# A hybrid trunk layer in two passes over its tokens: a mixer step's pieces over more slots, a transposition behind the product's other riders, and the first pass's blocks of h split by VectorE alone

## What is computed

```python
h = rmsnorm(x, g_pre) * (1.0 + scale) + shift      # scale, shift, gate from c @ w_ada
p = h @ w_in                                       # 8704 output columns
# columns of p feed four token mixers, their gate paths and the merge gates
y_pool, y_hgrn, y_conv, y_diff = ...               # pooling, HGRN2 recurrence, short conv, differential attention
merged = sum(gates[b] * (y[b] @ w_merge[b]) for b in range(4))
x + gate * rmsnorm(merged @ w_out, g_post)
```

## Time and profile before

| what | value |
|---|---|
| median of 3 runs (2573.1 to 2575.48) | 2574.45 us |
| the profiled execution | 2568.26 us |
| its span, first to last instruction | 2566.5 us |
| mean granted clock of TensorE | 0.962 |
| TensorE busy | 2284.2 us (89%) |
| VectorE busy | 1689.7 us (66%) |
| ScalarE busy | 1259.9 us (49%) |
| GpSimd busy | 1093.9 us (43%) |

### The profile page before, as it was taken

One profiled execution on the slowest core, in us unless ns is written; L12 is line 12 of the kernel. 1 busy time (PEld: TensorE's weight loads), 2 busy tenths in 40 slices (PEclk: granted clock), 3 DMA queues, 4 the chain that ended last, 5 costly groups with the idle time before them and its releaser, 6 DMA issues. The chain is left out here.

```text
span 2566.5 us, 35701 instructions
## 1 busy us (share of the span) xinstructions
PE 2284.2 (89%) x11572; PEld 1859.2 (72%) x11572; DVE 1689.7 (66%) x2872; ACT 1259.9 (49%) x2634; POOL 1093.9 (43%) x883
## 2 busy tenths in 40 slices
PE   3599999999989999998999999999999965989898
PEld 2487777777767777776887888777777744767676
DVE  6776666658888785547777777588888735344442
ACT  3454555535554545445666666445555343434341
POOL 1513323225664654323334333366566425243343
PEclk6799999999999999999999999999999988999999
DMA  6467544334433436453424242343343266576582
GB/s 224 142 201 226 152 131 130 111 96 140 124 112 110 124 103 202 135 155 95 129 79 118 80 117 63 117 128 113 111 129 111 93 213 184 148 208 175 154 223 63
DMA packets 351328, 350.85 MB, mean 137 GB/s; under 512 B 25904, under 2 KB 277168, under 8 KB 350128
## 3 DMA queue, kind: packets, MB, share of 16 engines
q1 hardware_dynamic: 351152, 348.66, 46.0%
HBM read 242.15 MB, written 106.43 MB: 136 GB/s over the span
## 5 line engine op out<-in xcount | busy, mean ns | idle before, releaser
L1622 PE MATMUL gb<-h_hi,w_hi 128*128 128x512 f32 x1904 | 785.8, 413 | 89.1 <-DVE o L1207 53.5
L1624 PE MATMUL gb<-h_hi,w_lo 128*128 128x512 f32 x1904 | 756.3, 397 | 0.0
L1623 PE MATMUL gb<-h_lo,w_hi 128*128 128x512 f32 x1904 | 754.2, 396 | 0.0
L1197 DVE TENSOR_TENSOR w_lo<-w,w_hi 128x512 fp32r<-128x512 f32 x340 | 304.7, 898 | 298.9 <-ACT w_hi L902 298.0
L1622 PEld LDWEIGHTS gb<-h_hi,w_hi 128*128 128x128 f32 x1904 | 365.5, 192 | 175.6 <-issue 98.6
L1624 PEld LDWEIGHTS gb<-h_hi,w_lo 128*128 128x128 f32 x1904 | 364.1, 191 | 80.5
L1623 PEld LDWEIGHTS gb<-h_lo,w_hi 128*128 128x128 f32 x1904 | 366.0, 192 | 66.5
L988 ACT ACTIVATE C_prob<-C_sc,C_negm 128x512 f32<-128x512 f32 (+3 forms) x320 | 198.8, 623 | 270.4 <-DVE C_negm L1290 269.0
L781 POOL TENSOR_TENSOR C_prob<-C_prob,C_cf 128x512 f32<-128x512 f32 (+3 forms) x160 | 161.3, 1027 | 344.3 <-DVE C_cf L1312 330.0
L918 ACT ACTIVATE o<-gb 128x512 f32<-128x512 f32 x272 | 161.3, 593 | 268.5 <-PE gb L1624 255.5
L902 ACT ACTIVATE w_hi<-w 128x512 fp32r<-128x512 f32 x340 | 212.0, 625 | 100.1 <-PE gb L1624 98.9
(11 more groups left out here) (231 smaller groups left out, 4118.2 us busy)
## 6 DMA issues: line engine op xcount, KB each, us to landing
w<-in_w_in_dram SPq DMA_DIRECT2D x136, 512.0 KB, 4.1
gT_scratch<-o SPq DMA_DIRECT2D x128, 256.0 KB, 2.8
D_gate<-gT_scratch SPq DMA_DIRECT2D x32, 1024.0 KB, 9.8
pT_scratch<-o SPq DMA_DIRECT2D x80, 256.0 KB, 2.9
C_qt<-qB_scratch SPq DMA_DIRECT2D x128, 128.0 KB, 2.9
C_ks<-kT_scratch SPq DMA_DIRECT2D x48, 256.0 KB, 4.8
A_x_all<-in_x_dram SPq DMA_DIRECT2D x16, 512.0 KB, 6.9
A_ada<-in_w_ada_dram SPq DMA_DIRECT2D x8, 1024.0 KB, 12.1
```

The source lines that it names most:

```text
L1197: tt(w_lo[n % RING][:, :, :], source(n), w_hi[n % RING][:, :, :].bitcast(F32), ALU.subtract).then_inc(wlo, 1)
L1622: mm(to, hi[:, k, :], h_hi[j][:, k, :], start=(fresh and k == 0), stop=False, skip_group_check=True)
L1623: mm(to, hi[:, k, :], h_lo[j][:, k, :], start=False, stop=False, skip_group_check=True)
L1624: last = mm(to, lo[:, k, :], h_hi[j][:, k, :], start=False, stop=(k == KH - 1), skip_group_check=True)
```

## The change

Three places are edited.

1. Mixers. `distances_x` is cut in two pieces and each runs over two slots (-7 and -6; -3 and -2); `decays_first` becomes two pieces at -4 and -3; `sigmoids` loses its last four scalings, which become `affine` at -10; the pooling sigmoid moves ahead of it. `level_decays` of the second head pair goes from -2 to -1, `query_decays` and `decays_second` from -1 to 0, `decay_queries` from 0 to 1, `advance_state` from 10 to 11, `pool_out` from 10 to 12 and its store from 11 to 13.
2. `turn_back` of the first half stands behind `values` and `turn`.
3. In the first half ScalarE evicts h11, h12 and h22, VectorE h21; VectorE makes all of t1 to t4 and all seven low parts, in the order 0, 1, 2, 3, 5, 4, 6; GpSimd does nothing for h. The products' own order stays.

```diff
+FIRST_ORDER = (0, 1, 2, 3, 5, 4, 6)
+
+EVICT_V = ((4, 5, 6, 7), (0, 1, 2, 3, 8, 9, 10, 11))
+EVICT_A = ((0, 1, 2, 3, 8, 9, 10, 11, 12, 13, 14, 15), (4, 5, 6, 7, 12, 13, 14, 15))
...
+
+        def hi_count(half, j, kk):
+            return 2 * (PER * half + (j if half else FIRST_ORDER.index(j))) + kk + 1
+
+        def lo_count(half, j, kk):
+            if half == 0:
+                return h_lo_v, hi_count(0, j, kk)
+            if j in LOW_BY_VECTOR:
+                return h_lo_v, 2 * (PER + LOW_BY_VECTOR.index(j)) + kk + 1
+            return h_lo_p, 2 * LOW_BY_POOL.index(j) + kk + 1
...
                     store_y(i, 4, yc, yc_ready, yc_stored)
-                i = mix_step(n, 11)
+                i = mix_step(n, 13)
                 if i is not None:
...
@@ -837,15 +859,6 @@
             sum_s3_s1(0)
             sum_s2(0)
             sum_s4(0)
-            for kk in range(2):
-                low(1, kk, 0, operand_part(1, kk))
-            for kk in range(2):
-                t3(0, kk)
-            for j in LOW_BY_POOL[1:]:
-                for kk in range(2):
-                    if j == 4:
-                        pool.wait_ge(t3_made, kk + 1)
...
                     pool_part(i)
-                i = mix_step(n, -1)
+                i = mix_step(n, 0)
                 if i is not None:
...
-                link(a(k_s[i % 2][:, :, :], in3[i % 2][:, 2:4, :], ACT.Sigmoid, scale=-1.0))
+                a(k_s[i % 2][:, :, :], in3[i % 2][:, 2:4, :], ACT.Sigmoid, scale=-1.0)
+                link(a(q_s[i % 2][:, :, :], in3[i % 2][:, 0:2, :], ACT.Sigmoid))
+
+            def affine(i):
+
                 for t in range(2):
                     a(f_s[:, t, :], f_s[:, t, :], ACT.Identity, scale=omlb[:, t:t + 1], bias=lb[:, t:t + 1])
-                    a(k_s[i % 2][:, t, :], k_s[i % 2][:, t, :], ACT.Copy, scale=omlb[:, t:t + 1])
-                a(q_s[i % 2][:, :, :], in3[i % 2][:, 0:2, :], ACT.Sigmoid).then_inc(sig_ready, 1)
+                for t in range(2):
+                    ins = a(k_s[i % 2][:, t, :], k_s[i % 2][:, t, :], ACT.Copy, scale=omlb[:, t:t + 1])
+                ins.then_inc(sig_ready, 1)
+
+            def pool_sigmoid(i):
...
@@ -1087,13 +1102,13 @@
                 root_x(0, t)
             for n in range(LEAD):
                 high(n)
-            for kk in range(2):
-                high_h(0, kk)
-            for q in range(4, 8):
+            act.wait_ge(mod_ready, 1)
+            for q in range(4):
                 evict(0, q)
-            for kk in range(2):
-                high_h(1, kk)
-            for q in range(12, 16):
+            for j in range(2):
+                for kk in range(2):
+                    high_h(j, kk)
+            for q in range(8, 16):
                 evict(0, q)
             for kk in range(2):
...
                     for kk in range(2):
-                        high_h(3 + n, kk)
+                        high_h(FIRST_ORDER[3 + n], kk)
                 for b, off in OUT_SLOT.items():
...
                 if i is not None:
+                    pool_sigmoid(i)
                     sigmoids(i)
+                i = mix_step(n, -10)
+                if i is not None:
+                    affine(i)
                 i = mix_step(n, 5)
...
                     key_decays(i)
-                for t, off in enumerate((-5, -2)):
+                for t, off in enumerate((-5, -1)):
                     i = mix_step(n, off)
                     if i is not None:
                         level_decays(i, t)
-                i = mix_step(n, -1)
+                i = mix_step(n, 0)
                 if i is not None:
...
 
-            def distances_x(i, t):
+            def distances_x(i, t, y0, y1):
                 dve.wait_ge(scanned, i + 1)
                 if i:
                     dve.wait_ge(r_done, 4 * (i - 1) + 2 * t + 2)
-                for y, m in enumerate(LEVELS):
+                for y in range(y0, y1):
+                    m = LEVELS[y]
                     v = b_s[:, t, :].rearrange("p (n u) -> p n u", u=2 * m)
                     to = X[:, t, y, :].rearrange("p (n u) -> p n u", u=2 * m)
                     ins = tt(to, v, v[:, :, m - 1:m].to_broadcast([P, P // (2 * m), 2 * m]), ALU.subtract)
                 link(ins)
+                if y1 < NL - 1:
+                    return
                 flat = X[:, t, 0:NL - 1, :]
                 stt(flat, flat, -1.0, flat, ALU.mult, ALU.min).then_inc(spread, 1)
...
             dve.wait_ge(mod_ready, 1)
-            for q in range(4):
+            for q in range(4, 8):
                 evict(0, q)
-            for kk in range(2):
-                low_h(0, kk, 0, operand_part(0, kk))
-            for q in range(8, 12):
-                evict(0, q)
+            for j in range(2):
+                for kk in range(2):
+                    low_h(j, kk, 0, operand_part(j, kk))
             for kk in range(2):
...
                     for kk in range(2):
-                        low_h(3, kk, 0, operand_part(3, kk))
-                if n == 1:
+                        t3_first(kk)
+                if n == 2:
                     for kk in range(2):
                         t4(0, kk)
-                if n == 3:
+                if n < 4:
+                    j = FIRST_ORDER[3 + n]
                     for kk in range(2):
-                        low_h(6, kk, 0, operand_part(6, kk))
+                        low_h(j, kk, 0, operand_part(j, kk))
...
                     scan(i)
+                i = mix_step(n, -7)
+                if i is not None:
+                    distances_x(i, 0, 0, 3)
                 i = mix_step(n, -6)
                 if i is not None:
-                    distances_x(i, 0)
+                    distances_x(i, 0, 3, NL - 1)
                 i = mix_step(n, -5)
                 if i is not None:
                     decay_keys(i)
                 i = mix_step(n, -4)
                 if i is not None:
-                    decays_first(i)
+                    decay_first_queries(i)
                 i = mix_step(n, -3)
                 if i is not None:
-                    distances_x(i, 1)
-                i = mix_step(n, 10)
+                    decay_first_keys(i)
+                    distances_x(i, 1, 0, 2)
+                i = mix_step(n, -2)
+                if i is not None:
+                    distances_x(i, 1, 2, NL - 1)
+                i = mix_step(n, 11)
                 if i is not None:
                     advance_state(i)
+                i = mix_step(n, 12)
+                if i is not None:
                     pool_out(i)
                 i = mix_step(n, 14)
                 if i is not None:
                     finish(i)
-                i = mix_step(n, 0)
+                i = mix_step(n, 1)
                 if i is not None:
                     decay_queries(i)
...
             def attention_behind(half, s):
-                i = None if half else finished(half, s, ON)
-                if i is not None:
-                    turn_back(i)
                 z = piece(half, s, VALUES)
                 if z is not None:
                     values(z)
                 z = piece(half, s, TURN)
                 if z is not None:
                     turn(z)
+                i = None if half else finished(half, s, ON)
+                if i is not None:
+                    turn_back(i)
 
```

80 lines of the change are left out of this document (37 added, 43 removed).

## The result

The changed kernel takes 2553.23 us (median of 4 runs, 2548.87 to 2558.27) against 2574.97 for the kernel before (4 runs, 2573.1 to 2577.0). The ratio is 0.9916, 95% interval 0.9896 to 0.9936: 22 us faster, where 44 were forecast (2530), and inside the range of 2507 to 2556. Measured again beside two experiments the ratio is 0.9903 (0.9885 to 0.9920), 25 us. In what follows a ratio is turned into microseconds with 2574, and an interval of 0.002 either side is 5 us.

What follows compares the result with a forecast made beforehand. TensorE's order of products was taken as the bound, with VectorE close behind in the mixers. Start -7, transposition -18 and mixers -20 (-16, -6, +7, -5) sum to -45: 2530 us from the median, range 2507 to 2556.

Steps and rivals of the forecast that it cites:

- the transposition's: First half's attention: values and turn matmuls run ahead of the transposition, covering 17.8 of 25.2 us of C_on waits; -18 us.
- VectorE's bunch: Mixers: add_out goes ahead of the two updates of S, so waits at products go; -6 us.
- ScalarE's group: Mixers, products base + 3 and base + 4: four scalings moved behind the next copy_out and high shorten waits; -16 us.
- the start: First half's h: VectorE takes GpSimd's work without a longer chain, and t2 begins earlier; -7 us, from -10 to -2.
- the state: Mixers: S comes a slot later while TensorE's norms stay, and query_decays starts later; +7 us.
- The estimate drawn from the rule: Start: if each of GpSimd's three sums blocked VectorE for its full length, the gain would be about -6 us.
- The rival that the wait comes back: Attention: the transposition's wait returns at the next product or the scores, 0 in place of -18: 2548 us; chance 0.09.
- Its sign: Attention: the prediction is wrong if the waits for C_on have only changed their names.
- The four waits for VectorE: Mixers, products base + 3 and base + 4: 6.9 us of waits for VectorE, delayed by ScalarE's high weights; gain 2 us.
- the seven waits for ScalarE: Mixers, products base + 3 and base + 4: 17.5 us of waits, each shrinking by up to 1.75, 11.0 us together.
- The slower rival: Mixers: the state becomes the bound, norms waiting 3 us in each of 16 steps, +55 us: 2582; chance 0.05.
- The clock: Mixers: long TensorE waits drop the clock for a while; if a quarter of the drops go, -5 of 23 us.

Runs made afterwards that it cites:

- gate_out served early: Changed kernel with the first half's gate_out put ahead of the low part of the weights: ratio 0.9860, 36 us faster than before; with the transposition back, 21 us.
- the group alone: Changed kernel with gate_out led forward; of the mixers' edits only the sigmoids in one slot and four scalings in the next: ratio 0.9834, 43 us faster than before.
- the cut distances: Changed kernel with gate_out led forward, mixers with sigmoids and scalings apart, distances in two pieces, no later slots: ratio 0.9905, 24 us faster than before.
- the later slots: Changed kernel with gate_out led forward and all mixer edits, later slots included: ratio 0.9860, 36 us faster than before; without the later slots, 24 us.
- Left at slot 10: Changed kernel with gate_out led forward, all mixer edits but advance_state back at slot 10: ratio 0.9830, 44 us faster than before.
- the mixers alone: Kernel before with only edit 1, the mixers' edits: ratio 0.9980, 5.1 us faster than before.
- the mixers as before: Changed kernel with gate_out led forward and all the mixers' edits taken out: ratio 0.9869, 34 us faster than before.

## Why the prediction was off by half

**Direction, and the range.** Faster was given 0.92, and 2553 lies at the edge of the range. Of the six terms two failed in their mechanism, the transposition's (-18) and that of VectorE's bunch (-6); ScalarE's group (-16) was right in part, and the start (-7) and the state (+7) came near.

**Start: mis-sized, -7, measured -9.7 at product 10.** The steps were right: t2's beginning came 3.8 us earlier where 2.8 were reckoned, and from there to the end of the last low part it is 24.0 us where 25.9 were. The sums cost t4 2.2 us and one low part of weights 0.5, 2.7 together for the 3 reckoned; the 1 us for a rounding in between did not arise, as VectorE has no idle time there. The estimate drawn from the rule of the Trainium skill's page SBUF — State Buffer (Who interferes with whom), -6, was further off. Product 4 starts at 90.56, not near 93.

**Transposition: failed.** The step is "Neither needs C_on ... so nothing else is late by it: gate_out, which needs the result, comes a step later". That the riders cover the wait was right to the hundredth in the step shown (1.21 left) and roughly in sum (5.3 left, 7.4 forecast). But `values` needs the gate_out of two units earlier, which is in the code and in no row: before, that wait never ended last, as the transposition ahead of it on TensorE waited for something that VectorE makes later. As the change was written, the term measures 3.9 us; with gate_out served early, 15 (36 against 21 by the runs). The rival that the wait comes back had this shape, but at the next product or at the scores, and with a chance of 0.09. Its sign was listed, too: 15.7 of the 19.9 us saved at C_on only changed their name.

**ScalarE's group: the sum of its waits as forecast, by another way.** ScalarE's waits fell by 15.9 us for the 16 forecast, but only in the kernel with all of the mixers' edits. The step that was off is "The four waits for VectorE gain less, 2 us". With the group alone the seven waits for ScalarE shrink by 6.8 us, of the 11 reckoned for the scalings, while VectorE's waits rise by 7.9: at product 146, base + 4, VectorE is waited for 2.43 us where there was no wait. That the runs are 9 us faster all the same (two intervals of about 5 us stand against each other) isn't explained by the waits.

**VectorE's bunch: failed.** The step is "The pieces moved on VectorE cost nothing by themselves: as many instructions of the same shapes". All five waits that the term looked at did go (2.97 at product 178 and its like are not in the trace after), 11.3 us where 6 were counted. But VectorE's waits in all rose by 3.8 us with the mixers' edits alone: the pieces moved into the slots of GpSimd's sums grew from 0.21 to 0.87 us each, and add_out was late at other products, 154, 202, 384 and 434 (12.2 us in the trace after). By the runs the cut distances cost 18 us before the later slots gave 12 back. The forecast knew this contention, priced it for the start from the earlier trace rows, and did not ask for it in the mixers, where it is as easily seen (S in the earlier trace rows, 4.04 us, for 0.61 where GpSimd is idle, as in the row at 677.53). That add_out is late in other slots instead was listed as what would prove it wrong, and it is what happened.

**The state: +7 forecast, +8.7 in waits.** The size was right and the reason only half: it isn't merely a slot later, it goes along with decays_second and so stays beside it. Left at slot 10, where decays_second is no longer, the two updates take 0.61 us again in step 2 and it is worth 8 us. The slower rival (2582) asked for 3 us in 16 steps; there were 10 or 11 waits of 1.1 us on average.

**The clock.** Forecast -5, and not measured by itself. From before to after the mean granted clock in the two stretches is 0.97 to 0.97 and 0.97 to 0.99. But the profiled execution of the changed kernel has the highest clock of nine: 0.973, where the nine average 0.965, against 0.960 in 23 executions of the kernel before. What comes with a pair of new waits is seen from product 145 to 165, the kernel before first, then the mixers alone (busy sum and count by engine, clock, DMA share, GB/s):

```profile
666.90:739.90 73.00, 70.26 (x386) 56.46 (x387) 63.05 (x120) 36.42 (x66) 39.66 (x41) 0.98 0.37 113
```

```profile
667.10:748.10 81.00, 73.69 (x386) 58.10 (x387) 64.93 (x115) 37.27 (x69) 41.24 (x47) 0.94 0.33 102
```

The same 20 products take 8 us longer, with waits of 3.16 us at product 146 and 3.47 at 154 that were not there; waits in all are 4.6 us more, and TensorE's own work is 3.4 us longer at a clock of 0.94 in place of 0.98. So nearly half of what this place lost was not in the waits, as far as one execution of each tells.

**What stays open.** Why the group alone makes the kernel faster although TensorE's waits don't shrink in sum; its executions average a granted clock of 0.967 (5) against 0.963 (4) with the mixers as before, and no run shows whether that is the reason. The later slots were not taken apart in runs: that `level_decays` gives most of theirs back is read from the waits. Nor was the start's second gain, of a better dealing of the evictions, measured apart from GpSimd's removal.

## What to carry to other kernels

When an instruction is moved behind others on its engine, list not only what it needs but everything that waits for what it releases, two buffers on, from the code: a wait that never ended last has no row. And when pieces are moved to a less busy slot of an engine, look at what the other engines do in that slot: here short VectorE instructions beside GpSimd's sums took four times their own length (0.87 us for 0.21), and the same pieces one slot earlier cost nothing that the runs can tell.

## What was not expected of the hardware

Who pays in the contention differs from place to place, and no run shows what decides it. In the start GpSimd's first sum took 3.32 us beside two low parts that kept their 1.18 each and a low part of weights that grew to 1.17, while t4 took 2.26 each beside sums of 1.56 and 2.14; in the mixers GpSimd's sums kept 1.26 to 1.74 and VectorE's subtractions took 0.87 instead of 0.21. The pair of VectorE's updates of S takes 0.61 us with GpSimd idle, 1.13 beside its small pooling pieces and 3.99 beside decays_second.
